# Expert gates on Trainium2: four fp32 one-hot products per group against twelve in bf16

## The chip, the cores and the metric

The kernel runs on one core of one Trainium2 chip. The metric is the time of one execution on the device in microseconds (us). Engines: TensorE (PE for matmuls, PEld for the loads of its stationary operand), VectorE (DVE), ScalarE (ACT), GpSimd (POOL), and SyncE (SP), whose queue issues most DMAs.

## The reference, cut to what matters

Two layers run over x (256 tokens by 1024). Each is an attention mixer followed by a retrieval among 16,384 = 128 x 128 experts. The retrieval, cut:

```
v1, i1 = top_k(sc[:, :, 0], 16)            # per token and head (8 heads)
v2, i2 = top_k(sc[:, :, 1], 16)
cand     = v1[..., :, None] + v2[..., None, :]
top_v, pos = top_k(cand, 16)
eidx     = i1 * 128 + i2 at pos
gates    = softmax(top_v)
a   = gelu(u_tab[eidx] . x) * gates
out = sum over the 8 x 16 chosen: a * v_tab[eidx]
```

The kernel gathers nothing. It multiplies every token with all 128 tiles of u, weights the result with a dense gate array, and multiplies with all 128 tiles of v. The gate array G[i2, i1, t] holds for each token t the gate of expert (i1, i2), and zero where that expert wasn't chosen. It is built as matrix products. For a token, the 128 choices (8 heads x 16) lie on the partitions. A matrix A[choice, n] = (n == one index of the choice) and a matrix B[choice, n] = gate of the choice where n == its other index give, as A transposed times B, the 128 x 128 gate block of that token.

## The kernel before, in words

Each layer ends in `experts(l)`. Its stages, in the order in which PE does them:

- Up products, 128 steps. Step n takes a tile of u (128 x 1024 fp32), which ACT copies in two halves into `hi` (rounded to fp32r, `split`, L967), and DVE subtracts to `lo` (`lower`, L1338). PE then does 24 products of 256 columns into one bank (`up`: hi by x_hi, hi by x_lo, lo by x_hi for each of 8 slices). ACT applies gelu into `work` (L973), and SP stores it to DRAM (`spill`). `hi` and `lo` have two slots each, so the split of step n+2 waits for the products of step n.
- During the steps up to 55, DVE finds the choices (`retrieve_head`, `choose`). After step 53, PE runs `picks`: 64 bf16 products that turn the indices so that choices lie on partitions (bank 6), and two fp32 transposes of the gates (bank 7). DVE copies these into `pick` (L1401, L1402): three rows of 256 tokens, fp32, for the two indices and the gate.
- Steps 56 to 119 each have a group of four tokens besides. DVE builds the one-hots of group g (`one_hot`, L1340): one TENSOR_TENSOR compares `iota` with the first index for four tokens (128 x 512, L1343), and four TENSOR_SCALAR, one a token, compare with the second index and multiply by the gate (128 x 128 each, L1346). It goes into one of two buffers `hot`. PE does the four fp32 products of the group after its up step (`group`, L747) into bank g % 4. ACT copies the bank into the gate array (`copy_gates`, L989). In DVE's program, a group stands after the two `lower` halves of a step. `one_hot(g)` waits until the products of group g-2 are done, `group(g)` waits for `hot_ready` g+1 and for the copy of group g-4.
- Steps 120 to 127 are up products alone. Then come the 128 down steps (`down`): weigh, split, and 12 products of 512 columns for a tile of v.

In the trace each fp32 product of a token shows as two matmul instructions with two weight loads: 1024 of them for 512 products. A product of fp32r or bf16 operands shows as one.

All three memory areas of the change lie in `wmod_ring` (3 x 1024 fp32 a partition). Its first two thirds are `hot`, its last third is first `pick` and later `back`, the area that fetches the stored gelu results once all 64 groups are done. In layer 0, it also takes tiles of w_mod before the groups begin and after they end.

The order is written out by hand: each engine has its own program, and semaphores tie them. `link` on DVE means that the next instruction waits for this one through a semaphore.

Of the kernel before, what the change touches and what calls it, by code (L numbers as in the profile page):

```python
# [8 lines left out]
ALU = mybir.AluOpType  # L9
# [3 lines left out]
BF16 = mybir.dt.bfloat16  # L13
# [3 lines left out]
P = 128  # L17
D = 1024
KT = D // P
T = 256  # L20
# [45 lines left out]
def win_cols(l):  # L66

    return QK_TILES[l] * KT * P + sum(V_WIDTHS[l]) * KT + (GATE_COLS * KT if l == 0 else 0)
# [11 lines left out]
KEYS_AT = QS_AT + 2 * 2 * T  # L80
OUT_AT = KEYS_AT
BIG = P * T
WIN_TILES = win_cols(1) // D
PIECE = D

# [65 lines left out]
def build(nc, a, out):  # L151

    with ExitStack() as ctx:
        def sb(name, shape, dt=F32):
            return ctx.enter_context(nc.sbuf_tensor(name, shape, dt))
# [3 lines left out]

        big = sb("big", [P, BIG])  # L160
        raw = sb("raw", [P, RAWS, D])
# [8 lines left out]
        wmod_ring = sb("wmod_ring", [P, MODS, D])  # L170
# [2 lines left out]
        c_all = sb("c_all", [P, D])  # L173
        work = sb("work", [P, 4, T])
        stat = sb("stat", [P, 256])
        pick = wmod_ring[:, 2, 0:3 * T].rearrange("p (a t) -> p a t", a=3)

        first_mods = [wmod_ring[:, n] for n in range(MODS)]
        first_mods += [big[:, V_AT + n * D:V_AT + (n + 1) * D] for n in range(TT)]
# [2 lines left out]
        first_mods += [big[:, n * D:(n + 1) * D] for n in range(LATE_MODS)]  # L182
        fox_maps = wmod_ring[:].rearrange("p a n -> p (a n)")

        hot = [x.rearrange("p (a t n) -> p a t n", a=2, n=P) for x in (wmod_ring[:, 0], wmod_ring[:, 1])]
        back = wmod_ring[:, 2].rearrange("p (r t) -> p r t", t=T)
        bank = [ctx.enter_context(nc.psum_tensor(f"bank{i}", [P, 512], F32)) for i in range(8)]

# [2 lines left out]
        iota = cst[:, C_IOTA:C_IOTA + P]  # L191
# [64 lines left out]
        def q_area(at, size, **kw):  # L256
# [48 lines left out]
                 "map_ps", "map_max", "neg_ready", "exp_done", "prob_ready", "pt_ps", "pt_copied", "av_ps", "av_copied",  # L305
                 "y_ps", "x_mixed",
                 "q_ps", "q_copied", "key_ps", "key_copied", "equal_ready", "sel_ready", "pick_copied",
                 "hot_ready", "hot_used", "g_copied", "hi_done", "lo_done", "w_used",
                 "s_gelu", "a_ready", "ah_done", "al_done",
                 "e_copied", "eT_ps", "x_done")  # L310
        s = [{n: sem(f"{n}_{l}") for n in names} for l in range(LAYERS)]
# [136 lines left out]
        def _(pool):  # L448
            for l in range(LAYERS):
# [26 lines left out]
                else:  # L476
                    pool.wait_ge(s[1]["wt_used"], 2 * WIN_TILES)
                pool.dma_start(big[:, WOUT_AT:WOUT_AT + KT * D], a["w_out"][l]).then_inc(wout_in, 16)
# [11 lines left out]
        def _(pe):  # L490
            def mm(o, w, x, start=True, stop=True, free=False):
                return nc.tensor.matmul(o, w, x, start=start, stop=stop, skip_group_check=free)  # L492
# [15 lines left out]
            def project_split():  # L508

                def open_half(w, h):  # L510
                    if h == 0 and w < QK_TILES[1] and w % 4 == 0:
                        pe.wait_ge(win_in[w // 4], loads_in(1, min(4, QK_TILES[1] - w) * D))
                    if h == 0 and w == QK_TILES[1]:
                        pe.wait_ge(win_in[4], loads_in(1, KT * V_WIDTHS[1][0]))
                    if h == 0 and w == WIN_TILES - 1:
                        pe.wait_ge(win_in[5], loads_in(1, KT * V_WIDTHS[1][1]))
# [213 lines left out]
            def experts(l):  # L730

                def up(n, r, wait=True):

                    if wait:
                        pe.wait_ge(s[l]["s_gelu"], n - 1)
                    o = bank[4 + r][:, 0:T]
                    for h in range(2):
                        pe.wait_ge(s[l]["hi_done"], 2 * n + h + 1)
                        pe.wait_ge(s[l]["lo_done"], 2 * n + h + 1)
                        for k in range(h * KT // 2, (h + 1) * KT // 2):  # L740
                            c = slice(k * P, (k + 1) * P)
                            mm(o, hi[:, r, c], x_hi[:, k, :], k == 0, False)
                            mm(o, hi[:, r, c], x_lo[:, k, :], False, False)
                            last = mm(o, lo[:, r, c], x_hi[:, k, :], False, k == KT - 1)
                        last.then_inc(s[l]["w_used"], 1)

                def group(g, b, wait=True):  # L747

                    if wait:
                        pe.wait_ge(s[l]["g_copied"], g - 3)  # L750
                    pe.wait_ge(s[l]["hot_ready"], g + 1)
                    for n in range(4):
                        last = mm(bank[b][:, n * P:(n + 1) * P], hot[b % 2][:, 0, n, :], hot[b % 2][:, 1, n, :])
                    last.then_inc(s[l]["hot_used"], 1)

                def down(j, r, first=False, end=False):

                    pe.wait_ge(s[l]["ah_done"], j + 1)
                    pe.wait_ge(s[l]["al_done"], j + 1)
                    for h in range(2):  # L760
                        pe.wait_ge(s[l]["hi_done"], STREAM + 2 * j + h + 1)
                        pe.wait_ge(s[l]["lo_done"], STREAM + 2 * j + h + 1)
                        c = slice(h * HALF, (h + 1) * HALF)
                        for t in range(TT):
                            o, tok = bank[2 * t + h][:, :], slice(t * P, (t + 1) * P)
                            mm(o, a_hi[:, r, tok], hi[:, r, c], first, False, True)
                            mm(o, a_hi[:, r, tok], lo[:, r, c], False, False, True)
                            last = mm(o, a_lo[:, r, tok], hi[:, r, c], False, end, True)
                        last.then_inc(s[l]["w_used"], 1)

                pe.wait_ge(s[l]["xh_done"], l + 1)
                pe.wait_ge(s[l]["xl_done"], l + 1)
                up(0, 0, False)
                up(1, 1, False)
                with pe.Fori(1, GROUP_AT // 2 - 1) as i:
                    for r in range(2):
                        up(2 * i + r, r)
                picks(l)
                for r in range(2):
                    up(GROUP_AT - 2 + r, r)  # L780
                for r in range(4):
                    up(GROUP_AT + r, r % 2)
                    group(r, r, False)
                with pe.Fori(1, GROUPS // 4) as i:
                    for r in range(4):
                        up(GROUP_AT + 4 * i + r, r % 2)
                        group(4 * i + r, r)
                with pe.Fori((GROUP_AT + GROUPS) // 2, NKEY // 2) as i:
                    for r in range(2):
                        up(2 * i + r, r)  # L790
                pe.wait_ge(s[l]["g_copied"], GROUPS)
                down(0, 0, first=True)
                with pe.Fori(0, NKEY // 2 - 1) as i:
                    for r in range(2):
                        down(2 * i + 1 + r, 1 - r)
                down(NKEY - 1, 1, end=True)
# [12 lines left out]
            for k in range(KT):  # L809
                last = mm(bank[1 + k // 4][:, (k % 4) * P:(k % 4 + 1) * P], silu8[:, k:k + 1].to_broadcast([P, P]), ident)  # L810
# [21 lines left out]
        def _(act):  # L832
# [101 lines left out]
            for l in range(LAYERS):  # L934
# [83 lines left out]
                act.wait_ge(s[l]["gate_max"], l + 1)  # L1018
                f(q_e[:], q_e[:], ACT.Exp).then_inc(s[l]["gate_exp"], 1)
                up_steps(32, GROUP_AT)  # L1020
                act.wait_ge(s[l]["pick_copied"], 2)
                with act.Fori(0, GROUPS // 4) as i:
                    for r in range(4):
                        up_step(GROUP_AT + 4 * i + r, r, i + GROUP_AT // 4)
# [25 lines left out]
        def _(dve):  # L1050
            steps = [0]

            def link(ins):
                steps[0] += 1
                ins.then_inc(dve_step, 1)
                dve.wait_ge(dve_step, steps[0])

            v = nc.vector
# [274 lines left out]
            def experts(l):  # L1333
# [6 lines left out]
                def one_hot(g, r, wait=True):  # L1340
                    if wait:
                        dve.wait_ge(s[l]["hot_used"], g - 1)
                    v.tensor_tensor(hot[r % 2][:, 0], iota.unsqueeze(1).to_broadcast([P, 4, P]),  # L1343
                                    pick[:, 0, bass.ds(4 * g, 4)].unsqueeze(2).to_broadcast([P, 4, P]), ALU.is_equal)
                    for n in range(4):
                        ins = v.tensor_scalar(hot[r % 2][:, 1, n, :], iota, pick[:, 1, bass.ds(4 * g + n, 1)],  # L1346
                                              pick[:, 2, bass.ds(4 * g + n, 1)], ALU.is_equal, ALU.mult)
                    ins.then_inc(s[l]["hot_ready"], 1)

                def weigh(j, b, round_):  # L1350
                    dve.wait_ge(s_in[b], 16 * (round_ + 1) + 16 * l * (NKEY // STAGES))
# [46 lines left out]
                for _ in left:  # L1398
                    pass
                dve.wait_ge(s[l]["pick_ps"], l + 1)  # L1400
                v.tensor_copy(pick[:, 0:2, :].rearrange("p a b -> p (a b)"), bank[6][:, :]).then_inc(s[l]["pick_copied"], 1)  # L1401
                v.tensor_copy(pick[:, 2, :], bank[7][:, 0:T]).then_inc(s[l]["pick_copied"], 1)  # L1402
                dve.wait_ge(s[l]["pick_copied"], 2)
                for g in range(4):
                    for half in range(2):
                        lower(GROUP_AT + g, g, half)
                    one_hot(g, g, g >= 2)
# [40 lines left out]


            dve.wait_ge(const_in, 16)  # L1450
            v.tensor_copy(ident_bf, ident).then_inc(ident_ready, 1)
            dve.wait_ge(silu_e, 1)
            link(v.tensor_scalar(silu8, silu8, 1.0, None, ALU.add))
# [6 lines left out]
            for l in range(LAYERS):  # L1460
# [14 lines left out]
                if l == 0:  # L1475
                    dve.wait_ge(par_in, 16)
                    for n in range(2):
                        ins = v.tensor_tensor_reduce(stat[:, n * HD:(n + 1) * HD], lam_in[:, 2 * n, :], lam_in[:, 2 * n + 1, :], 1.0, 0.0,
                                                     ALU.mult, ALU.add, lam[:, n:n + 1])
# [31 lines left out]
                for m in range(KT):  # L1511
                    dve.wait_ge(s[l]["eT_ps"], m // 2 + 1)
                    c = (m % 2) * T
# [97 lines left out]
```

## Time and profile before

| | |
|---|---|
| median of 3 runs | 2069.59 us (2067.72 to 2069.62) |
| profiled execution, its own time | 2068.17 us |
| its span, first to last instruction | 2066.2 us |
| PE busy | 2001.3 us (97%) |
| DVE busy | 1488.5 us (72%) |
| ACT busy | 1054.0 us (51%) |
| granted TensorE clock, mean | 0.981 |

The span is what the profiler sees of the instructions, 2.0 us less than the execution's own time. A busy share is an average over the whole span. "x" numbers are counts of instructions. In a timeline the first column is the start in us, the second the length from the start of the first to the end of the last of a merged row. Matmuls are pipelined, so their lengths overlap and what a matmul costs PE is the distance between two starts.

### The profile page before, as it was taken

The page shows a single profiled execution, that of the slowest core. Times are in us where ns is not written, and L with a number is a line of the kernel's source. Part 1 is how long each engine was busy: PE and PEld are TensorE (multiplying, and loading weights), DVE is VectorE, ACT ScalarE, POOL GpSimd, SP SyncE. Part 2 cuts the span into 40 slices and gives each one's busy share as a digit, 9 for nine tenths or more (in the row PEclk, how much of TensorE's full clock was granted, in tenths as well). Part 3 has the DMA queues.
Part 4 walks back from the last instruction along what each step waited for, and adds up shares of the span by engine and source line. Part 5 has one row for each costly group of instructions (what it writes and reads, how often), then busy time and mean ns, then how long its engine had stood idle before and what let it go on. Part 6 is the DMA issues. An engine that isn't in the chain of part 4 may idle for free.

```text
span 2066.2 us, 43340 instructions
## 1 busy us (share of the span) xinstructions
PE 2001.3 (97%) x12616; PEld 1792.2 (87%) x12616; DVE 1488.5 (72%) x3743; ACT 1054.0 (51%) x2059; POOL 27.7 (1%) x56
## 2 busy tenths in 40 slices
PE   5989999999999999999999899999999999999997
PEld 4847899999999877777779689999999998888886
DVE  5663778877777688888875348886777767777776
ACT  2032245755555555555554423566555555555554
POOL 0000000000000000000000000000000000000000
PEclk7999999999999999999989999999999999999999
DMA  9861279865556899999830324877565677777774
GB/s 377 333 234 42 101 272 288 254 192 174 171 176 177 269 329 327 317 333 321 279 106 31 153 106 125 228 219 214 176 174 170 176 207 244 240 241 241 241 241 152
DMA packets 170903, 446.77 MB, mean 216 GB/s; under 512 B 19024, under 2 KB 85840, under 8 KB 166880
## 3 DMA queue, kind: packets, MB, share of 16 engines
q1 hardware_dynamic: 163472, 392.65, 60.0%
q0 software_dynamic: 7376, 53.45, 6.7%
q8 instruction: 27, 0.44, 0.1%
q14 instruction: 28, 0.23, 0.0%
HBM read 409.32 MB, written 36.70 MB: 216 GB/s over the span
## 4 chain that ended last, share of the span: by engine, by line
PE 94%; ACT 2%; DVE 2%; DMA 1%; issue 1%; DVEq 0%; ACTq 0%; SPq 0%
PE bank L492 93%; ACT big L913 1%; DMA big<-in_w_mod 1%; PE bank L626 1%; DVE raw L1079 0%; DVE big L1174 0%; DVE big L1096 0%; DVE wmod_ring L1096 0%; DVE x_lo L1088 0%; ACT hi L871 0%; ACT L973 0%; ACT big L931 0%; DMA cst<-in_consts 0%; PE bank L803 0%; ACT raw L860 0%
## 5 line engine op out<-in xcount | busy, mean ns | idle before, releaser
L1338 DVE TENSOR_TENSOR lo<-raw,hi 128x512 fp32r<-128x512 f32 x1024 | 702.8, 690 | 346.6 <-ACT hi L967 342.3
L967 ACT ACTIVATE hi<-raw 128x512 fp32r<-128x512 f32 x1024 | 642.6, 629 | 445.3 <-PE bank L492 433.2
L492 PE MATMUL bank<-x_hi,hi 128*128 128x256 f32 x2152 | 623.1, 290 | 3.6 <-ACT work L973 1.6
L492 PE MATMUL bank<-x_hi,lo 128*128 128x256 f32 x2152 | 610.7, 284 | 0.0
L492 PE MATMUL bank<-x_lo,hi 128*128 128x256 f32 x2152 | 606.2, 283 | 0.0
L492 PEld LDWEIGHTS bank<-x_hi,hi 128*128 128x128 f32 x2152 | 414.1, 192 | 6.4 <-issue 4.5
L492 PEld LDWEIGHTS bank<-x_hi,lo 128*128 128x128 f32 x2152 | 414.3, 193 | 0.0
L492 PEld LDWEIGHTS bank<-x_lo,hi 128*128 128x128 f32 x2152 | 411.8, 192 | 0.0
L492 PE MATMUL bank<-hi,a_hi 128*128 128x512 f32 x1024 | 401.1, 392 | 3.4 <-issue 2.1
L492 PE MATMUL bank<-hi,a_lo 128*128 128x512 f32 x1024 | 398.8, 389 | 0.0
L492 PE MATMUL bank<-lo,a_hi 128*128 128x512 f32 x1024 | 398.6, 389 | 0.0
L492 PE MATMUL bank<-raw,big 128*128 128x256 f32 (+1 forms) x1040 | 238.8, 388 | 17.8 <-ACT raw L860 17.8
L492 PEld LDWEIGHTS bank<-raw,big 128*128 128x128 f32 (+1 forms) x1040 | 196.4, 192 | 50.4 <-issue 22.6
L492 PEld LDWEIGHTS bank<-hi,a_hi 128*128 128x128 f32 x1024 | 192.2, 188 | 54.5 <-issue 13.3
L492 PEld LDWEIGHTS bank<-hi,a_lo 128*128 128x128 f32 x1024 | 192.2, 188 | 40.5
L492 PEld LDWEIGHTS bank<-lo,a_hi 128*128 128x128 f32 x1024 | 192.2, 188 | 39.0
L973 ACT ACTIVATE work<-bank 128x256 f32<-128x256 f32 x256 | 98.1, 383 | 188.0 <-PE bank L492 186.9
L1346 DVE TENSOR_SCALAR wmod_ring<-cst,wmod_ring 128x128 f32<-128x128 f32 x512 | 142.4, 342 | 0.0
L492 PE MATMUL bank<-wmod_ring 128*128 128x128 f32 x1024 | 135.1, 275 | 0.0
L492 PEld LDWEIGHTS bank<-wmod_ring 128*128 128x128 f32 x1024 | 125.7, 192 | 0.0
L995 ACT ACTIVATE a_hi<-wmod_ring 128x256 fp32r<-128x256 f32 x256 | 103.5, 404 | 11.4 <-DVE wmod_ring L1352 10.6
L1352 DVE TENSOR_TENSOR wmod_ring<-wmod_ring,big 128x256 f32<-128x256 f32 x256 | 107.2, 419 | 1.8 <-issue 0.4
(157 smaller groups left out, 1305.3 us busy)
## 6 DMA issues: line engine op xcount, KB each, us to landing
raw<-in_u SPq DMA_DIRECT2D x256, 512.0 KB, 3.9
raw<-in_v SPq DMA_DIRECT2D x256, 512.0 KB, 4.6
s_store<-work SPq DMA_DIRECT2D x256, 128.0 KB, 3.7
wmod_ring<-s_store SPq DMA_DIRECT2D x256, 128.0 KB, 3.7
wmod_ring<-in_w_mod SPq DMA_DIRECT2D x54, 512.0 KB, 5.8
big<-in_w_mod SPq DMA_DIRECT2D x40, 512.0 KB, 6.2
big<-in_w_q POOLq DMA_DIRECT2D x16, 1024.0 KB, 6.3
big<-in_w_in POOLq DMA_DIRECT2D x6, 2048.0 KB, 13.4
```

Source lines behind the costliest of these rows:

```text
L492: return nc.tensor.matmul(o, w, x, start=start, stop=stop, skip_group_check=free)
L626: last = nc.tensor.transpose(bank[4 + n % 2][:, c * P:(c + 1) * P], scores[:, i, c * P:(c + 1) * P], ident)
L913: last = f(c, c, ACT.Exp, bias=neg[:, 2 * i + t:2 * i + t + 1], accum_out=den[:, 2 * i + t:2 * i + t + 1])
L967: f(hi[:, r % 2, c], raw[:, r, c], ACT.Copy).then_inc(s[l]["hi_done"], 1)
L973: f(work[:, r, :], bank[4 + r % 2][:, 0:T], ACT.Gelu).then_inc(s[l]["s_gelu"], 1)
L995: f(a_hi[:, r % 2, :], back[:, b, :], ACT.Copy).then_inc(s[l]["ah_done"], 1)
L1338: v.tensor_tensor(lo[:, r % 2, c], raw[:, r, c], hi[:, r % 2, c].bitcast(F32), ALU.subtract).then_inc(s[l]["lo_done"], 1)
L1346: ins = v.tensor_scalar(hot[r % 2][:, 1, n, :], iota, pick[:, 1, bass.ds(4 * g + n, 1)], pick[:, 2, bass.ds(4 * g + n, 1)], ALU.is_equal, ...
L1352: v.tensor_tensor(back[:, b, :], back[:, b, :], gates[:, bass.ds(j, 1), :].rearrange("p a t -> p (a t)"), ALU.mult)\
```

## The change

A gate value is cut into three bf16 pieces whose sum is the fp32 value: its bf16 rounding, the bf16 rounding of what is left, and what is left then. The one-hots (zeros and ones) are bf16. B becomes three bf16 matrices, one a piece, and the block of a token is the sum of three bf16 products in one bank. So a group has 12 bf16 products in place of 4 in fp32.

The buffer of a group is laid out as [5 matrices][128 indices n][4 tokens], with the four tokens innermost. Both operands of each product are therefore read with a step of four elements, 8 bytes. VectorE builds it with two instructions: one compares a table `iota4` (each index four times) with both indices of the four tokens (128 x 1024, output bf16), the other multiplies the second one-hot by the three pieces (128 x 1536, bf16). The second reads what the first wrote, so it waits for it (`hot_plain`).

Once a layer, before the groups: the pick copy now writes bf16, and the pieces take two subtractions and three roundings of 256 columns, each waiting for the one before it where it reads its output. ACT, ahead of its first group, waits for one more count of `pick_copied`. Once in the kernel, at the very start, `iota4` is written (128 x 512, bf16).

```
@@ -80,6 +80,7 @@
 OUT_AT = KEYS_AT
 BIG = P * T
+HOT = 5 * 4 * P // 2
 WIN_TILES = win_cols(1) // D
@@ -173,7 +174,11 @@
         stat = sb("stat", [P, 256])
-        pick = wmod_ring[:, 2, 0:3 * T].rearrange("p (a t) -> p a t", a=3)
+        iota4 = sb("iota4", [P, P, 4], BF16)
+        pick_bf = sb("pick_bf", [P, 2, T], BF16)
+        ring = wmod_ring[:].rearrange("p a n -> p (a n)")
+        gate_bf = ring[:, 2 * HOT:2 * HOT + 3 * T // 2].bitcast(BF16).rearrange("p (a t) -> p a t", a=3)
+        gate_left = ring[:, 0:T]
@@ -182,7 +187,7 @@
-        hot = [x.rearrange("p (a t n) -> p a t n", a=2, n=P) for x in (wmod_ring[:, 0], wmod_ring[:, 1])]
+        hot = [ring[:, n * HOT:(n + 1) * HOT].bitcast(BF16).rearrange("p (a n t) -> p a n t", a=5, t=4) for n in range(2)]
@@ -305,7 +310,7 @@
-                 "hot_ready", "hot_used", "g_copied", "hi_done", "lo_done", "w_used",
+                 "hot_plain", "hot_ready", "hot_used", "g_copied", "hi_done", "lo_done", "w_used",
@@ -750,7 +755,8 @@
                     for n in range(4):
-                        last = mm(bank[b][:, n * P:(n + 1) * P], hot[b % 2][:, 0, n, :], hot[b % 2][:, 1, n, :])
+                        for c in range(3):
+                            last = mm(bank[b][:, n * P:(n + 1) * P], hot[b % 2][:, 0, :, n], hot[b % 2][:, 2 + c, :, n], c == 0, c == 2)
                     last.then_inc(s[l]["hot_used"], 1)
@@ -1018,7 +1024,7 @@
-                act.wait_ge(s[l]["pick_copied"], 2)
+                act.wait_ge(s[l]["pick_copied"], 3)
@@ -1340,12 +1346,13 @@
                 def one_hot(g, r, wait=True):
                     if wait:
                         dve.wait_ge(s[l]["hot_used"], g - 1)
-                    v.tensor_tensor(hot[r % 2][:, 0], iota.unsqueeze(1).to_broadcast([P, 4, P]),
-                                    pick[:, 0, bass.ds(4 * g, 4)].unsqueeze(2).to_broadcast([P, 4, P]), ALU.is_equal)
-                    for n in range(4):
-                        ins = v.tensor_scalar(hot[r % 2][:, 1, n, :], iota, pick[:, 1, bass.ds(4 * g + n, 1)],
-                                              pick[:, 2, bass.ds(4 * g + n, 1)], ALU.is_equal, ALU.mult)
-                    ins.then_inc(s[l]["hot_ready"], 1)
+                    v.tensor_tensor(hot[r % 2][:, 0:2], iota4[:].unsqueeze(1).to_broadcast([P, 2, P, 4]),
+                                    pick_bf[:, :, bass.ds(4 * g, 4)].unsqueeze(2).to_broadcast([P, 2, P, 4]), ALU.is_equal)\
+                        .then_inc(s[l]["hot_plain"], 1)
+                    dve.wait_ge(s[l]["hot_plain"], g + 1)
+                    v.tensor_tensor(hot[r % 2][:, 2:5], hot[r % 2][:, 1:2].to_broadcast([P, 3, P, 4]),
+                                    gate_bf[:, :, bass.ds(4 * g, 4)].unsqueeze(2).to_broadcast([P, 3, P, 4]), ALU.mult)\
+                        .then_inc(s[l]["hot_ready"], 1)
@@ -1398,9 +1405,14 @@
                 dve.wait_ge(s[l]["pick_ps"], l + 1)
-                v.tensor_copy(pick[:, 0:2, :].rearrange("p a b -> p (a b)"), bank[6][:, :]).then_inc(s[l]["pick_copied"], 1)
-                v.tensor_copy(pick[:, 2, :], bank[7][:, 0:T]).then_inc(s[l]["pick_copied"], 1)
+                v.tensor_copy(pick_bf[:].rearrange("p a b -> p (a b)"), bank[6][:, :]).then_inc(s[l]["pick_copied"], 1)
+                v.tensor_copy(gate_bf[:, 0, :], bank[7][:, 0:T]).then_inc(s[l]["pick_copied"], 1)
                 dve.wait_ge(s[l]["pick_copied"], 2)
+                v.tensor_tensor(gate_left, bank[7][:, 0:T], gate_bf[:, 0, :], ALU.subtract).then_inc(s[l]["pick_copied"], 1)
+                dve.wait_ge(s[l]["pick_copied"], 3)
+                link(v.tensor_copy(gate_bf[:, 1, :], gate_left))
+                link(v.tensor_tensor(gate_left, gate_left, gate_bf[:, 1, :], ALU.subtract))
+                link(v.tensor_copy(gate_bf[:, 2, :], gate_left))
@@ -1448,6 +1460,7 @@
             dve.wait_ge(const_in, 16)
+            v.tensor_copy(iota4[:], iota.unsqueeze(2).to_broadcast([P, P, 4]))
             v.tensor_copy(ident_bf, ident).then_inc(ident_ready, 1)
```

## Rows read from the trace of the kernel before

**Rows 1.** The page: busy time of each engine, and the chain's shares by engine

```profile
PE 2001.3 (97%) x12616; PEld 1792.2 (87%) x12616; DVE 1488.5 (72%) x3743; ACT 1054.0 (51%) x2059; POOL 27.7 (1%) x56
...
PE 94%; ACT 2%; DVE 2%; DMA 1%; issue 1%; DVEq 0%; ACTq 0%; SPq 0%
```

**Rows 2.** Windows: stretch, its length, busy PE, PEld, DVE, ACT, POOL, PEclk, DMA, GB/s

```profile
436.40:682.20 245.80, 245.80 (x2089) 245.80 (x2089) 187.25 (x445) 138.88 (x262) 0.00 (x0) 1.00 0.60 175
1430.80:1676.60 245.80, 245.80 (x2089) 245.80 (x2089) 190.03 (x453) 137.88 (x259) 0.00 (x0) 1.00 0.60 174
```

**Rows 3.** PE's timeline over one step with its group

```profile
560.77 1.06 PE L492 MATMUL bank<-wmod_ring 128*128 128x128 f32 x8
561.58 0.36 PE L492 MATMUL bank<-x_hi,hi 128*128 128x256 f32 x1
561.78 0.28 PE L492 MATMUL bank<-x_lo,hi 128*128 128x256 f32 x1
561.90 0.28 PE L492 MATMUL bank<-x_hi,lo 128*128 128x256 f32 x1
...
564.54 1.06 PE L492 MATMUL bank<-wmod_ring 128*128 128x128 f32 x8
```

**Rows 4.** PE and its weight loads by shape, whole span: count | busy us, mean ns

```profile
L492 PE MATMUL bank<-wmod_ring 128*128 128x128 f32 x1024 | 135.1, 275 | 0.0
L492 PEld LDWEIGHTS bank<-wmod_ring 128*128 128x128 f32 x1024 | 125.7, 192 | 0.0
...
L492 PE MATMUL bank<-par,big 128*128 128x128 bf16 x128 | 7.5, 219 | 0.0
L492 PEld LDWEIGHTS bank<-par,big 128*128 128x128 bf16 x128 | 7.2, 98 | 0.1
```

**Rows 5.** PE's timeline over the picks of layer 0

```profile
424.02 3.75 PE L492 MATMUL bank<-par,big 128*128 128x128 bf16 x64
427.61 0.39 PE L727 MATMUL bank<-cst,big 128*128 128x128 f32 x2
```

**Rows 6.** DVE's timeline over one step with its group

```profile
561.91 0.69 DVE L1338 TENSOR_TENSOR lo<-raw,hi 128x512 fp32r<-128x512 f32 x1 [0.76 <-ACT hi L967]
562.51 0.68 DVE L1343 TENSOR_TENSOR wmod_ring<-cst,wmod_ring 128x512 f32<-128x512 f32 x1
563.12 1.11 DVE L1346 TENSOR_SCALAR wmod_ring<-cst,wmod_ring 128x128 f32<-128x128 f32 x4
564.14 0.69 DVE L1338 TENSOR_TENSOR lo<-raw,hi 128x512 fp32r<-128x512 f32 x1
```

**Rows 7.** DVE by shape: the nearest rows to the two new instructions

```profile
L1324 DVE TENSOR_TENSOR big<-big 128x512 bf16<-128x512 bf16 x32 | 21.9, 684 | 0.0
L1502 DVE TENSOR_TENSOR x_lo<-raw,x_hi 128x2048 fp32r<-128x2048 f32 x2 | 4.6, 2291 | 5.1 <-ACT x_hi L960 5.1
L1310 DVE CAST big<-big 128x512 f32<-128x512 uint32 x2 | 0.8, 421 | 0.0
```

**Rows 8.** DVE's timeline around the pick copy of layer 0

```profile
428.03 0.69 DVE L1401 COPY wmod_ring<-bank 128x512 f32<-128x512 f32 x1 [2.19 <-PE bank L727]
428.64 0.41 DVE L1402 COPY wmod_ring<-bank 128x256 f32<-128x256 f32 x1
430.20 0.69 DVE L1338 TENSOR_TENSOR lo<-raw,hi 128x512 fp32r<-128x512 f32 x1 [1.15 <-ACT hi L967]
```

**Rows 9.** The start of the kernel: timeline of DVE and PE

```profile
3.69 0.23 DVE L1451 CAST par<-cst 128x128 bf16<-128x128 f32 x1 [3.69 <-DMA cst<-in_consts]
3.83 0.16 DVE L1453 TENSOR_SCALAR stat<-stat 128x8 f32<-128x8 f32 x1
4.03 0.20 DVE L1454 RECIPROCAL stat<-stat 128x8 f32<-128x8 f32 x1
4.26 0.17 DVE L1455 TENSOR_TENSOR stat<-stat 128x8 f32<-128x8 f32 x1
```

**Rows 10.** Window: a stretch of up steps without groups, layer 1

```profile
1330.00:1420.00 90.00, 89.20 (x744) 89.03 (x743) 68.34 (x136) 61.12 (x106) 0.00 (x0) 1.00 0.78 224
```

## The prediction

> **What bounds the kernel now.** I read the page first for the engine that carries the chain [rows 1]: PE is busy 97% of the span and 94% of the chain is its. A share over the whole span doesn't say that the stage of the groups is like that, so next come the windows over the two layers' group stages [rows 2]: PE is busy in all of 245.80 us of each, at the full granted clock (1.00), while DVE is busy 76 to 77%, ACT 56% and the DMA engines 60%. In this stage nothing but the distance between PE's starts counts. PE's timeline gives it [rows 3]: groups begin at 560.77 and 564.54, a period of 3.77 us. The 24 products of an up step start 0.12 us apart (561.78, 561.90), 2.88 us in all. The rest, 3.767 - 2.88 = 0.887 us, is the group. It holds eight fp32 instructions. The merged row is 1.06 us long and one is 275 ns [rows 4], so they start (1.06 - 0.275) / 7 = 0.112 us apart, and eight make 0.90. The reader is to see that 0.887 is this and nothing else: no idle time stands ahead of the group or behind it. There are 64 such groups a layer, 128 in all: 114 us of the kernel.
>
> **PE, the term that decides.** Removed: 128 x 0.887 us. Added: 12 bf16 products of 128 columns a group. The trace has the same shape in one place, the picks: 64 products in a merged row of 3.75 us [rows 5], each 219 ns long [rows 4], so (3.75 - 0.219) / 63 = 0.056 us from start to start, each with its own weight load (98 ns, against 192 ns for one in fp32 [rows 4]). Twelve make 0.673 us. There the operands lie packed. Here both step by 8 bytes, and no row shows a strided read by PE. Its bounds: 0.056 us if the step is free, and from the nearest slower row 0.112 us, as if each column took the two passes' time that it takes in fp32.
>
> I take 0.056. The products of the up step, fp32r, already read 4 bytes a column at one column per PE cycle (256 columns in 0.120 us), and a bf16 weight load is far shorter than the fp32 one. So there is some room on both reads, but how much isn't shown, and this is the weakest step. By the Trainium skill, page "Advanced Engine Details and Errata", section "SBUF Cachelines", SBUF is read in lines of 16 bytes, and two hits in a line are enough to hide the access: with 8 bytes a step there are just two, so by it the step is free and the sum stays at 0.673 us, at the very edge of the rule. No row here shows it.
>
> Another page speaks against the change. The Trainium skill, "TensorE: Matmul & The Clock Gate", section "Back-to-back issue gap", gives about 81 ns a matmul for a stream of weight load and matmul pairs of 128 columns. By that, twelve would take 0.97 us and the kernel would get slower by some 11 us. The row of the picks, 56 ns with a load each [rows 5], disagrees.
>
> There is a seam besides. The first product of the next up step needs a weight load of 192 ns, and ahead of it now stands a short product instead of an fp32 one. Below: nothing, as at the old seam, where the block's 0.887 us is less than eight times 0.112. Above: what the fp32 load is longer than the bf16 one, 0.19 - 0.10 = 0.09 us. I take 0.03. The new block is then 0.70 us, the period 3.58, and the saving 128 x (0.887 - 0.703) = 23.6 us; with the seam's two bounds it is 27.4 to 15.9 us.
>
> **DVE, which must stay below PE.** Its timeline [rows 6]: in a period two `lower` of 0.60 us start to start, one compare of 0.61, four TENSOR_SCALAR in 1.02, together 2.84 of 3.77 us, the rest idle behind ACT. So DVE's saving, if there is one, is worth nothing; what counts is whether the new pair stays under what PE leaves. The pair covers 1024 and 1536 elements. Bounds from rows: at one element a cycle, 2048 elements took 2291 ns and 512 took 684 [rows 7], that is 158 ns + 1.042 ns an element, so 1.225 and 1.758 us. At two a cycle, as the cast of 512 words in 421 ns shows the engine can go for one input (0.52 ns an element), 0.69 and 0.96 us. The second waits for the first through a semaphore: a linked instruction starts about 0.035 us after the end of the one before (3.83 + 0.16 to 4.03 [rows 9]), while an unlinked one starts 0.08 us before it. Per period:
>
> - two a cycle: 1.21 + 0.69 + 0.035 + 0.96 - 0.08 = 2.82 us, hidden under 3.58;
> - one a cycle: 1.21 + 1.225 + 0.035 + 1.758 - 0.08 = 4.15 us, over both the new and the old period.
>
> The nearest row, L1324, is a TENSOR_TENSOR with bf16 output and runs at one a cycle (684 ns for 512), but its second input, `numbers`, is fp32 in the code. Here all three are 2 bytes and the innermost run has step 1. Two such elements are the 4 bytes which each stream already moves a cycle in the fp32 rows (512 in 0.68 us [rows 6]), so no more bytes pass than the rows show. I take two a cycle, with both ends kept. The Trainium skill says the same on page "VectorE: DVE Perf Modes", section "The perf-mode tier table": TENSOR_TENSOR doubles its rate with bf16 operands in SBUF and not with fp32 ones; by it the first of the two sums holds. If only the second instruction ran at one a cycle, the sum would be 1.21 + 0.73 + 1.68 = 3.62 us: PE would wait 0.04 us a group and most of the gain would stay.
>
> **Waits and queues.** Behind the new wait on DVE stand the second instruction and then the `lower` of the next step. `hot_ready` comes two groups ahead of its use (DVE had finished a group at 564.23, and PE takes that one some 4 us later, the next but one [rows 3, 6]), and the `lower` has to be done only two steps after the slot came free. ACT does the same two splits, one gelu and one bank copy, 56% of 3.77 us, 2.1 us a period [rows 2]. SP issues the same DMAs, now every 3.58 us, which raises their rate from 175 to some 184 GB/s. A stretch of bare up steps moves 224 GB/s with PE 99% busy [rows 10], so the loads follow.
>
> **Once a layer.** The pick copy [rows 8] takes 428.03 to 429.05. With the subtractions and roundings, four more of at most 0.42 us and 0.035 each, DVE is done near 430.9. The next `lower`, which starts at 430.20, slips 0.7 us. Its step's products start at 436.47 - 2.88 = 433.6 us, two us after it then ends. Cost zero; without that cover 1.9 us a layer. ACT reaches the wait for `pick_copied` 3 only after step 55, long past 430.
>
> **Once in the kernel.** `iota4` stands ahead of the cast and of the three small instructions that PE waits for [rows 9]. 512 elements: 0.34 to 0.61 us start to start (from 421 and 684 ns less 0.08). The queue of w_mod tiles behind may take in some of it. I take +0.4; bounds 0 and 0.6.
>
> **Sum.** 2068.17 (this execution's own time) - 23.6 + 0.4 = 2045.0 us. The median of the runs is 1.4 us above the profiled execution, so I forecast 2046 us. Within this case the seam and the start give 2041 to 2055.
>
> **Rivals.**
>
> - Strided reads cost PE the second cycle a column, 0.112 us a product. The block is 12 x 0.112 = 1.35 us, 0.46 more than now, over 128 groups +59 us: 2129. Decisive point: 0.887 / 12 = 0.074 us a product is break-even; above it the kernel is slower. For it: no strided read in the trace, both operands at once strided. Against: bf16 columns are half as wide as those that PE streams at full rate. Chance 0.14.
> - Something between, 0.06 to 0.081 us a product: loads that no longer fully hide, or a step that costs a part. At 0.065 it is 2060 with the seam, at 0.081, the figure of the page named above, 2081 without it: +10.9. Chance 0.13, of which 0.06 is faster, 0.03 within the bound of no change and 0.04 slower.
> - DVE runs one element a cycle in both instructions and sets the period at 4.15 us: (4.15 - 3.767) x 128 = +49, 2119. It decides from a DVE sum of 3.77 us. For it: the row of L1324. Against: its fp32 input. Chance 0.06.
> - The forecast, PE at 0.056 and DVE hidden: chance 0.67.
>
> That PE isn't the limit and the change therefore moves nothing I exclude by [rows 2].
>
> **How the numbers follow.** Faster: 0.67 + 0.06 = 0.73. Within 0.2% (4 us, about what a measurement of this kernel can tell from no change): 0.03. Slower: 0.04 + 0.14 + 0.06 = 0.24. The range leaves out the two slow rivals, together 0.20, and so runs from 2039 (the whole seam gone, and a little) to 2085 us. The likeliest case's own is 2041 to 2055.
>
> **What would show it.** In the new profile's PE timeline a merged row of 12 bf16 products would be (0.219 + 11 x 0.056) = 0.84 us long, groups 3.58 us apart, and the stage 229 us a layer in place of 241. A row of 1.45 us and a period of 4.2 would be the strided read. DVE: the group of the compare at 0.69 us and of the multiply at 0.96 us; at 1.2 and 1.76 us it is the third rival, with PE then waiting for DVE's `wmod_ring` in each group. The window's clock should stay at 1.00. The forecast falls if PE starts are spaced above 0.074 us, or if idle time shows ahead of the group.

## The result, and the profile after

The changed kernel takes 2133.26 us (median of 4 runs, 2132.36 to 2134.36) against 2068.91 us before: a ratio of 1.031, with a 95% interval of 1.0295 to 1.0325. It is 64 us slower. The profiled execution took 2132.36 us with a span of 2130.4 us.

The page first, as in [rows 1], then the window over the groups of layer 0, as in [rows 2]:

```profile
PE 2068.4 (97%) x13128; PEld 1851.6 (87%) x13128; DVE 1494.4 (70%) x3368; ACT 1055.1 (50%) x2059; POOL 27.7 (1%) x56
...
436.40:711.20 274.80, 274.80 (x2305) 270.86 (x2305) 186.08 (x254) 136.70 (x256) 0.00 (x0) 1.00 0.52 154
```

PE is still busy without a gap in the stage of the groups and at the full granted clock (1.00). VectorE is busy for less of it than before (186.08 of 274.80 us). So nothing new waits: the same engine has more to do. Its timeline over one step, against [rows 3]:

```profile
560.95 0.28 PE L497 MATMUL bank<-x_hi,lo 128*128 128x256 f32 x1
561.08 1.58 PE L497 MATMUL bank<-wmod_ring 128*128 128x128 bf16 x12
562.41 0.37 PE L497 MATMUL bank<-x_hi,hi 128*128 128x256 f32 x1
562.62 0.28 PE L497 MATMUL bank<-x_lo,hi 128*128 128x256 f32 x1
...
565.38 1.58 PE L497 MATMUL bank<-wmod_ring 128*128 128x128 bf16 x12
```

The groups begin 4.30 us apart, not 3.77. The block is 4.30 - 2.88 = 1.42 us, against 0.887. By shape, to be held against [rows 4]:

```profile
L497 PE MATMUL bank<-wmod_ring 128*128 128x128 bf16 x1536 | 202.5, 296 | 0.0
...
L497 PEld LDWEIGHTS bank<-wmod_ring 128*128 128x128 bf16 x1536 | 163.4, 118 | 7.7
```

The merged row gives (1.58 - 0.296) / 11 = 0.117 us from start to start. The bf16 product of the picks, same shape and type but packed operands, took 219 ns and 0.056 from start to start [rows 4, 5]. Each product is longer by 77 ns and each weight load by 20 ns. From these rows alone either could set the pace.

VectorE's timeline over a step, against [rows 6]:

```profile
562.21 0.69 DVE L1344 TENSOR_TENSOR lo<-raw,hi 128x512 fp32r<-128x512 f32 x1 [1.02 <-ACT hi L973]
562.82 0.68 DVE L1349 TENSOR_TENSOR wmod_ring<-iota,pick_bf 128x1024 bf16<-128x1024 bf16 x1
563.64 0.96 DVE L1353 TENSOR_TENSOR wmod_ring<-wmod_ring 128x1536 bf16<-128x1536 bf16 x1
564.80 0.69 DVE L1344 TENSOR_TENSOR lo<-raw,hi 128x512 fp32r<-128x512 f32 x1 [0.20 <-ACT hi L973]
```

1024 elements in 0.68 us and 1536 in 0.96: two elements a cycle, and VectorE waits more than before ahead of `lower`. The pick copy, against [rows 8], and the start, against [rows 9]:

```profile
428.04 0.69 DVE L1408 CAST pick_bf<-bank 128x512 bf16<-128x512 f32 x1 [2.19 <-PE bank L732]
...
430.34 0.29 DVE L1415 CAST wmod_ring<-wmod_ring 128x256 bf16<-128x256 f32 x1
430.67 0.69 DVE L1344 TENSOR_TENSOR lo<-raw,hi 128x512 fp32r<-128x512 f32 x1
```

```profile
3.75 0.43 DVE L1463 CAST iota<-cst 128x512 bf16<-128x512 f32 x1 [3.75 <-DMA cst<-in_consts]
...
4.67 0.17 DVE L1468 TENSOR_TENSOR stat<-stat 128x8 f32<-128x8 f32 x1
```

The `lower` behind the picks starts at 430.67 in place of 430.20, and the first group still begins at 436.5. The start is 0.41 us later at this point and nothing of it is left at the first group.

From the first to the last product of the groups, layer 0 takes 271.9 us (436.5 to 708.4) against 238.1, layer 1 272.0 (1469.7 to 1741.7) against 238.1. That is +67.7 us, and the span grew by 64.2. Of the other 3.5 us, 3.2 came back between the two stages: from the last product of layer 0's groups to the first of layer 1's it was 764.5 us (674.6 to 1439.1), and it is 761.3 (708.4 to 1469.7). Some 2 us of them lie before the end of layer 0's down steps (the last copy of layer 0's output by ACT starts 31.75 us later than before, where the groups had left a lag of 33.8). There PE is idle for 3.5 us before (712.0 to 1058.4) and for 1.6 after (746.0 to 1090.2). Up to that copy every run below is shorter than the kernel before as well, by 1.2 us in run 8 and by 2.1 or 2.2 in the others, with packed operands too. So against the one trace of before this part goes with the change and not with the step of the reads. The prediction has no term for it, and its cause stays open. The rest varies from run to run.

### The profile page after: what moved, and what is told of

Read it like the earlier page. It is cut to its first block, busy times and chain, and to the rows that moved or that the text cites. A ratio compares the mean times of both kernels' runs of the same rounds, so it can differ in the third digit from the quotient of the medians.

```text
span 2130.4 us, 43749 instructions
## 1 busy us (share of the span) xinstructions
PE 2068.4 (97%) x13128; PEld 1851.6 (87%) x13128; DVE 1494.4 (70%) x3368; ACT 1055.1 (50%) x2059; POOL 27.7 (1%) x56
## 4 chain that ended last, share of the span: by engine, by line
PE 94%; ACT 2%; DVE 1%; DMA 1%; issue 1%; SPq 0%; ACTq 0%; DVEq 0%
PE bank L497 93%; ACT big L919 1%; DMA big<-in_w_mod 1%; PE bank L631 1%; DMA raw<-in_v 0%; DVE raw L1085 0%; DVE big L1180 0%; DVE big L1102 0%; DVE wmod_ring L1102 0%; DVE x_lo L1094 0%; ACT hi L877 0%; ACT L979 0%; DMA cst<-in_consts 0%; ACT big L937 0%; PE bank L809 0%
## 5 line engine op out<-in xcount | busy, mean ns | idle before, releaser
L497 PE MATMUL bank<-wmod_ring 128*128 128x128 bf16 x1536 | 202.5, 296 | 0.0
L497 PEld LDWEIGHTS bank<-wmod_ring 128*128 128x128 bf16 x1536 | 163.4, 118 | 7.7
L1353 DVE TENSOR_TENSOR wmod_ring<-wmod_ring 128x1536 bf16<-128x1536 bf16 x128 | 122.6, 958 | 17.4
L995 ACT ACTIVATE big<-bank 128x512 f32 x128 | 76.7, 599 | 75.2 <-PE bank L497 75.2
```

The source lines that it names most:

```text
L995: f(dst, bank[b][:, :].rearrange("p (t j) -> p j t", t=4), ACT.Copy).then_inc(s[l]["g_copied"], 1)
L1353: v.tensor_tensor(hot[r % 2][:, 2:5], hot[r % 2][:, 1:2].to_broadcast([P, 3, P, 4]), gate_bf[:, :, bass.ds(4 * g, 4)].unsqueeze(2).to_broa ...
```

## The experiments

**What the experiments change.** Where a run is said to have wrong values, the products read other addresses of the same buffer, so the gate array isn't the reference's; instructions, counts, shapes and waits stay. An operand with a step of 8 or 16 elements, and the moving one in layer 0 of run 7, is read from one place in all products of a group. Runs 2, 3 and 5 to 8 are one execution each; what is read from them are distances and clocks within a trace. One helper serves them (`flat` is the buffer of a group as 2560 bf16 elements):

```
+        def cut(b, at, step):
+            return flat[b][:, at:at + step * P].rearrange("p (n t) -> p n t", t=step)[:, :, 0] if step > 1 else flat[b][:, at:at + P]
```

**1. Both operands packed.**

```
-  last = mm(bank[b][:, n * P:(n + 1) * P], hot[b % 2][:, 0, :, n], hot[b % 2][:, 2 + c, :, n], c == 0, c == 2)
+  last = mm(bank[b][:, n * P:(n + 1) * P], cut(b % 2, n * P, 1), cut(b % 2, 1024 + n * P, 1), c == 0, c == 2)
```

> Both operands of the 12 bf16 products are read packed (128 adjacent elements of the same buffer), so the gate array holds wrong values; everything else is as in the changed kernel. Theory S (the 8-byte step of the operands is the whole loss): products 0.056 us apart as in the picks, a block of 0.67 to 0.76 us, groups 3.58 us apart, total near 2045 us, faster than before by about 24. Rival C (the loss lies in the products' number, in the three that accumulate into the same columns, or in their place between fp32r products, not in the step): blocks stay at 1.42 us, total near 2132.

Measured: 2045.57 us, ratio to the kernel before 0.9889 (0.9873 to 0.9906). PE's timeline:

```profile
562.40 0.84 PE L501 MATMUL bank<-wmod_ring 128*128 128x128 bf16 x12
563.06 0.36 PE L501 MATMUL bank<-x_hi,hi 128*128 128x256 f32 x1
...
566.02 0.84 PE L501 MATMUL bank<-wmod_ring 128*128 128x128 bf16 x12
```

One product is 220 ns in this stage, so (0.84 - 0.220) / 11 = 0.056 us. The groups stand 3.62 us apart. The step of the operands is the whole loss, and more: without it the change wins 23 us. Rival C is out. In this run the three products of a token read the same elements; run 4 will show the same pace with three different pieces.

**2. One operand packed at a time.** Same edit, with steps (1, 4) for (stationary, moving) in layer 0 and (4, 1) in layer 1.

> One operand packed at a time, values wrong for it: in layer 0 the stationary operand is packed and the moving one keeps its 8-byte step; in layer 1 it is the other way round. Theory M (the moving read sets the pace): groups 4.30 us apart in layer 0 and 3.58 in layer 1. Theory W (the weight load sets it): 3.58 in layer 0 and 4.30 in layer 1. If either step alone is enough, 4.30 in both and a total near 2132; else near 2089.

Measured: 2086.14 us. PE's timeline, layer 0 and then layer 1, and the shapes in a window of each:

```profile
563.83 1.55 PE L501 MATMUL bank<-wmod_ring 128*128 128x128 bf16 x12
...
1560.59 0.86 PE L501 MATMUL bank<-wmod_ring 128*128 128x128 bf16 x12
...
1564.21 0.86 PE L501 MATMUL bank<-wmod_ring 128*128 128x128 bf16 x12
```

```profile
L501 PE MATMUL bank<-wmod_ring 128*128 128x128 bf16 x593 | 76.7, 293 | 0.0
L501 PEld LDWEIGHTS bank<-wmod_ring 128*128 128x128 bf16 x591 | 62.0, 113 | 2.2
...
L501 PE MATMUL bank<-wmod_ring 128*128 128x128 bf16 x564 | 40.5, 221 | 0.0
L501 PEld LDWEIGHTS bank<-wmod_ring 128*128 128x128 bf16 x564 | 33.2, 115 | 2.0
```

With the moving operand alone at 8 bytes, a product starts every (1.55 - 0.293) / 11 = 0.114 us. With the stationary one alone, every (0.86 - 0.221) / 11 = 0.058, and the period is 3.62 us. Theory M holds. It isn't quite all: with both at 8 bytes a product took 0.117 us, and the groups of layer 0 took 271.9 us against 269.2 here (436.2 to 705.4). So of the 0.061 us that a product lost, 0.058 belong to the moving operand, and the stationary one's step costs the other 2.7 us a layer. The load takes 113 ns in the first case too, where its operand is packed: so its extra length isn't its own step alone.

**3. Steps of 4 and of 16 bytes, both operands.** Steps (2, 2) in layer 0, (8, 8) in layer 1.

> Both operands read at a step of two elements (4 bytes) in layer 0 and of eight (16 bytes) in layer 1, values wrong. Theory N (a step of one 4-byte word is free, a longer one costs): groups 3.58 us apart in layer 0. Theory A (any step but one costs the double): 4.30 in layer 0. Layer 1: if the cost is a fixed doubling, 4.30; if it grows with the bytes stepped over, a product takes twice 0.117 us, 12 of them 2.8 us, and the groups stand about 5.7 us apart.

Measured: 2243.27 us. PE's timeline in layer 0, then in layer 1, and the windows over part of layer 1's groups, over one block and over the up products behind it:

```profile
562.94 0.86 PE L501 MATMUL bank<-wmod_ring 128*128 128x128 bf16 x12
...
1562.11 3.00 PE L501 MATMUL bank<-wmod_ring 128*128 128x128 bf16 x12
1564.74 0.48 PE L501 MATMUL bank<-x_hi,hi 128*128 128x256 f32 x1
...
1566.57 0.41 PE L501 MATMUL bank<-x_hi,hi 128*128 128x256 f32 x1
1566.78 0.41 PE L501 MATMUL bank<-x_lo,hi 128*128 128x256 f32 x1
...
1569.31 3.00 PE L501 MATMUL bank<-wmod_ring 128*128 128x128 bf16 x12
```

```profile
1500.00:1700.00 200.00, 200.00 (x1054) 170.66 (x1053) 88.59 (x118) 62.72 (x118) 0.00 (x0) 0.81 0.32 95
...
1562.10:1564.70 2.60, 2.60 (x14) 1.66 (x12) 0.69 (x1) 0.91 (x2) 0.00 (x0) 1.00 0.00 0
...
1565.00:1569.20 4.20, 4.20 (x25) 4.20 (x23) 2.34 (x3) 1.23 (x2) 0.00 (x0) 0.59 0.55 156
```

At 4 bytes a product costs (0.86 - 0.219) / 11 = 0.058 us: theory N. At 16 bytes, one is 415 ns long and starts every (3.00 - 0.415) / 11 = 0.235 us: twice the cost at 8 bytes, as the growing version said. Its 5.7 us a period was too low: this period is 7.20 us (1562.11 to 1569.31), and the mean over layer 1 is 6.73 (64 groups, first to last product 1425.7 to 1852.2). The rest is in the up products behind the block: they start 0.21 us apart (1566.57 to 1566.78) for most of the step where they took 0.12 at the full clock. The granted clock of the stretch is 0.81, a mean over parts at 2.4 GHz and parts at 1.2 GHz: it is 1.00 in the block and 0.59 over the up products behind it. It fell although PE counts as busy throughout.

**4. Two tokens innermost: the version that follows.** The buffer is laid out as [10][128][2], and the pick copies write group by group so that VectorE still needs two instructions. It computes the reference.

```
-  hot: rearrange("p (a n t) -> p a n t", a=5, t=4)
+  hot: rearrange("p (a n t) -> p a n t", a=10, t=2)
-  hot[b % 2][:, 0, :, n],      hot[b % 2][:, 2 + c, :, n]
+  hot[b % 2][:, n // 2, :, n % 2], hot[b % 2][:, 4 + 2 * c + n // 2, :, n % 2]
-  v.tensor_tensor(hot[r % 2][:, 0:2], iota4 ... [P, 2, P, 4], pick_bf[:, :, bass.ds(4 * g, 4)] ...
+  v.tensor_tensor(hot[r % 2][:, 0:4], iota2 ... [P, 4, P, 2], pick_bf[:, bass.ds(8 * g, 8)] as [4][2] ...
```

(The table keeps its name `iota4` in the code and is half as long, `iota2` above. The multiply and the writes of the pieces are laid out alike and not shown.)

> Computes the reference. The buffer holds two tokens innermost instead of four, so both operands are read at a step of 4 bytes; VectorE still builds it in two instructions with innermost runs of two. Theory N: products 0.056 us apart, total 2045 us, faster than before. Theory A: total near 2132. VectorE: 0.69 and 0.96 us if runs of two keep two elements a cycle, else 1.2 and 1.76 us, which with fast products would give groups 4.15 us apart and 2117 us.

Measured: 2047.05 us, ratio 0.9896 (0.9879 to 0.9912). PE's and VectorE's timeline:

```profile
562.96 0.86 PE L498 MATMUL bank<-wmod_ring 128*128 128x128 bf16 x12
...
566.58 0.86 PE L498 MATMUL bank<-wmod_ring 128*128 128x128 bf16 x12
```

```profile
564.70 0.69 DVE L1350 TENSOR_TENSOR wmod_ring<-iota,pick_bf 128x1024 bf16<-128x1024 bf16 x1
565.55 0.96 DVE L1354 TENSOR_TENSOR wmod_ring<-wmod_ring 128x1536 bf16<-128x1536 bf16 x1 [0.16 <-DVE wmod_ring L1350]
```

Runs of two keep VectorE at two elements a cycle, and PE no longer pays. This is the change as it was forecast, in the layout that keeps it.

**5. The law of the moving read: 6 and 32 bytes.** Stationary packed, moving at 3 elements in layer 0 and 16 in layer 1.

> Stationary operand packed, moving operand at a step of three elements (6 bytes) in layer 0 and of sixteen (32 bytes) in layer 1, values wrong. So far moving steps of 4, 8 and 16 bytes gave 0.058, 0.114 and 0.235 us a product. Theory R (the time goes with the bytes stepped over, about 0.44 ns for 4 bytes): 0.086 us in layer 0 and 0.47 in layer 1. Theory L (the time goes with the 16-byte lines touched, at most one a column, 1.8 ns each): also 0.086 in layer 0, but 0.235 again in layer 1. Rival D (free up to 4 bytes, then double and double again): 0.114 in layer 0.

Measured: 2211.36 us. PE's timeline, layer 0, layer 1:

```profile
563.41 1.23 PE L501 MATMUL bank<-wmod_ring 128*128 128x128 bf16 x12
...
1562.26 2.94 PE L501 MATMUL bank<-wmod_ring 128*128 128x128 bf16 x12
```

One product is 252 and 410 ns long: (1.23 - 0.252) / 11 = 0.089 us, (2.94 - 0.410) / 11 = 0.230. Theory L. At 32 bytes it costs no more than at 16. At 0.089 the groups of layer 0 stand 3.96 us apart, against 3.77 before the change.

**6. The stationary operand at 16 and 32 bytes,** moving packed.

> Moving operand packed, stationary operand at a step of eight elements (16 bytes) in layer 0 and of sixteen (32 bytes) in layer 1, values wrong. At 8 bytes a load grew from 98 to 115 ns and stayed hidden (0.058 us a product). Theory H (the weight load reads several parts at once and hides at any step): 0.06 us in both layers, total near 2050. Rival: the load itself becomes the pace at 16 bytes, with products 0.08 us apart or more and groups over 3.9 us apart.

Measured: 2061.07 us, neither of the two. PE's timeline and the loads, layer 0, layer 1:

```profile
564.54 0.96 PE L501 MATMUL bank<-wmod_ring 128*128 128x128 bf16 x12
...
568.27 0.96 PE L501 MATMUL bank<-wmod_ring 128*128 128x128 bf16 x12
```

```profile
L501 PEld LDWEIGHTS bank<-wmod_ring 128*128 128x128 bf16 x636 | 43.7, 149 | 2.3
...
L501 PEld LDWEIGHTS bank<-wmod_ring 128*128 128x128 bf16 x576 | 39.9, 150 | 2.1
```

The load grew to 149 ns and almost hides: a product starts every (0.96 - 0.230) / 11 = 0.066 us, the groups every 3.73. The total lies 11 us above what theory H said and well below the rival's.

**7. Is it the step, or the blocks of 16 bytes?** Runs of neighbours, one run in each 16 bytes: two columns a run in layer 0, four in layer 1.

```
+        def runs(b, at, run):
+            return flat[b][:, at:at + 8 * P // run].rearrange("p (n t) -> p n t", t=8)[:, :, 0:run]
...
+  x = runs(b % 2, 1024, 2) if l == 0 else runs(b % 2, 1024 + n * P, 4)
```

> Stationary operand packed; the moving operand's innermost step is one element, but its 128 columns are spread over 16-byte lines: 64 runs of two neighbours, one run a line, in layer 0, and 32 runs of four neighbours, one run a line, in layer 1. Values wrong. Theory L (a product costs 1.8 ns for each 16-byte line touched, and no less than 0.056 us): 64 lines give 0.114 us in layer 0, as the 8-byte step did, and 32 lines give 0.058 in layer 1. Rival E (what counts is whether neighbouring columns lie next to each other): 0.056 to 0.06 in both layers. Rival J (each jump costs, whatever it spans): 64 jumps cost 0.085 or so in layer 0 and 0.07 in layer 1.

Measured: 2087.88 us. PE's timeline, layer 0, layer 1:

```profile
560.90 1.55 PE L504 MATMUL bank<-wmod_ring 128*128 128x128 bf16 x12
...
1620.10 0.87 PE L504 MATMUL bank<-wmod_ring 128*128 128x128 bf16 x12
```

One product is 293 and 220 ns long: 0.114 and 0.059 us. Theory L again. Half of the neighbours adjacent doesn't help; how many 16-byte blocks the row of 128 columns touches does.

All moving reads together, stationary operand packed except at 4 bytes (run 3); "blocks" counts the 16-byte blocks touched:

| moving operand | blocks | us a product | 1.8 ns x blocks |
|---|---|---|---|
| packed | 16 | 0.056 | 0.029 |
| step 4 bytes | 32 | 0.058 | 0.058 |
| four neighbours in 16 bytes | 32 | 0.059 | 0.058 |
| step 6 bytes | 48 | 0.089 | 0.086 |
| step 8 bytes | 64 | 0.114 | 0.115 |
| two neighbours in 16 bytes | 64 | 0.114 | 0.115 |
| step 16 bytes (run 8) | 128 | 0.225 | 0.230 |
| step 32 bytes | 128 | 0.230 | 0.230 |

**8. Where the rest of the 7.2 us period came from.** Steps (8, 8) in layer 0, (1, 8) in layer 1.

> Both operands at a step of 16 bytes in layer 0, the moving one alone in layer 1 (stationary packed), values wrong. It asks where the unexpected part of the 7.2 us period came from that both gave in layer 1 before: there the granted clock fell to 0.81 and the up products ran at 0.21 us for half of the step. If that goes with the load of the stationary operand: layer 0 at 7.2 us a period with the clock near 0.8, layer 1 at 5.7 with the clock near 1.0, products 0.235 us apart in both. If it goes with the layer or with chance: layer 0 near 5.7, layer 1 near 7.2, or both alike.

Measured: 2401.57 us. Windows over the groups of layer 0 and of layer 1, and PE's timeline in layer 1:

```profile
436.40:860.00 423.60, 423.60 (x2239) 361.49 (x2238) 189.36 (x251) 133.02 (x250) 0.00 (x0) 0.81 0.33 97
1632.00:2008.00 376.00, 376.00 (x2259) 297.07 (x2258) 188.53 (x250) 133.38 (x250) 0.00 (x0) 0.92 0.38 110
```

```profile
1703.26 2.88 PE L501 MATMUL bank<-wmod_ring 128*128 128x128 bf16 x12
...
1708.86 2.88 PE L501 MATMUL bank<-wmod_ring 128*128 128x128 bf16 x12
1711.39 0.54 PE L501 MATMUL bank<-x_hi,hi 128*128 128x256 f32 x1
1711.72 0.42 PE L501 MATMUL bank<-x_lo,hi 128*128 128x256 f32 x1
...
1715.96 2.88 PE L501 MATMUL bank<-wmod_ring 128*128 128x128 bf16 x12
```

Both operands at 16 bytes give 0.81 in either layer. The moving one alone gives 0.92: a period is 5.60 us where the clock stays up (1703.26 to 1708.86), near the 5.7 expected, and 7.10 where it falls behind the block (1708.86 to 1715.96). So the extra time is the clock. It fell in the stages whose moving reads step by 16 or 32 bytes and stayed at 1.00 over the groups at every faster pace, and with the stationary operand's step it falls more often (0.81 against 0.92). In the changed kernel's groups it didn't fall (1.00). What in such reads lowers it, and why the stationary operand matters to it, stays open.

**9. Two pieces instead of three,** on top of run 4.

```
-                        for c in range(3):
+                        for c in range(2):
-                link(v.tensor_tensor(gate_left, gate_left, gate_bf[:, 1, :], ALU.subtract))
-                link(v.tensor_copy(gate_bf[:, 2, :], gate_left))
```

> The layout with two tokens innermost (4-byte step) and only two bf16 pieces of the gate instead of three, so the gate's last eight bits are left out: eight products a group. If the distance between PE's starts is still all that counts, four products of 0.058 us less in each of 128 groups save 30 us more: 2047 - 30 = 2017 us. Rival: VectorE or the splits take over as the limit of the stage, since the period would be 3.39 us; then less than 30, above all idle time of PE ahead of the up steps.

Measured: 2019.44 us, ratio 0.9758 (0.9745 to 0.9771).

```profile
561.02 0.63 PE L498 MATMUL bank<-wmod_ring 128*128 128x128 bf16 x8
...
564.42 0.63 PE L498 MATMUL bank<-wmod_ring 128*128 128x128 bf16 x8
```

The period is 3.40 us and PE still doesn't wait. The saving over run 4 is 27.6 us of the 30 expected. It is the fastest version, at the price of a gate that is rounded to two pieces.

## Why the prediction was wrong, step by step

- **The step that failed** is "I take 0.056": the cost of one bf16 product whose operands step by 8 bytes. It is 0.117 us, above even the upper bound of 0.112 that I had taken from the fp32 rows, and runs 1 and 2 put 0.058 of the 0.061 us between on the moving operand. Everything behind it follows: 12 x 0.117 = 1.40 us, a block of 1.42, and 128 x (1.42 - 0.887) = 68 us of loss in place of 23.6 of gain. The first rival had named the strided read and priced it at 2129 us; it got 0.14. Its price came near because the cost at 8 bytes happens to be the double: "the second cycle a column" isn't the mechanism, since 128 columns cost 0.058 us at 4 bytes and 0.235 at 16 (run 3).
- **The argument for it** was that fp32r products read 4 bytes a column at full rate, so a bf16 read had "some room". The room is there, but it is counted in 16-byte blocks touched, not in bytes used: 4 bytes a column, packed in fp32r or stepped in bf16, touch one block for four columns, and that is just free (0.058 us). 8 bytes touch twice as many, and that is double.
- **The rule that I leaned on beside it.** The Trainium skill, "Advanced Engine Details and Errata", section "SBUF Cachelines", says that at least two hits on a line are needed to absorb the access latency. I read it as: two are enough. The block of 16 bytes is confirmed (32 bytes cost the same as 16, run 5). Two hits weren't enough for the moving operand: 0.114 us against 0.056. Four were.
- **The rule that spoke against.** The 81 ns of the Trainium skill, "TensorE: Matmul & The Clock Gate", section "Back-to-back issue gap", isn't seen in any run here: packed pairs of load and product went at 0.056 us also between fp32r products (run 1).
- **Break-even** at 0.074 us left out the seam. With the seam as measured, 0.06 us, it is (0.887 - 0.06) / 12 = 0.069. At 0.066 the groups stood 3.73 us apart and the total was 2061 (run 6), below the kernel before; at 0.089 they stood 3.96 apart (run 5, layer 0), above the 3.77 before.
- **The seam** was taken as 0.03 us. In run 1 the block is 3.62 - 2.88 = 0.74 us and the products make 12 x 0.056 = 0.67, so it is some 0.06: inside the bounds, worth 4 us.
- **The total with packed operands** came out at 2045.6 us against the forecast of 2046 (run 1), and that is luck in part. Its groups saved 19.6 us (228.3 us a layer in place of 238.1) where the sum had 23.6. The span shrank by 23.9 us because of the 4.3 us outside the groups, 3.7 of them the gain between the two stages that stays unexplained.
- **The low end of 2041** leaves out the 1.4 us between the profiled execution and the median: 2068.17 - 27.4 + 1.4 = 2042. Nothing hangs on it.
- **VectorE** was right: 0.68 and 0.96 us against 0.69 and 0.96, two elements a cycle, hidden. The wait between them costs 0.14 us (562.82 + 0.68 to 563.64), not 0.035. It is hidden too.
- **Once a layer, once in the kernel:** DVE done at 430.6 against 430.9 predicted, no cost on the path. `iota4` 0.41 us at the start, taken as 0.4, but none of it is left at the first group.
- **What was wrong in the weighing:** the sign hung on the only step without a row, and the forecast still got 0.67. The steps with rows missed by little: 4 us at the seam, and a wait on VectorE that stayed hidden. The rival that this step left open cost two and a half times what the forecast won.

## What to carry to other kernels

A layout that pleases the engine that writes a buffer must be priced on the engine that reads it, and where that reader sets the end, its read comes first: here VectorE had 0.9 us of idle time a step to give, and PE none. Keep PE's moving operand at four or more columns per 16 bytes. Here, with 128 bf16 columns, a step was free up to that (0.058 us against 0.056), so two bf16 tokens interleaved serve both engines. If the step on which the sign depends has no row in the trace, look for what would be needed to stay clear of it, or give its bad end a larger chance.

## What the runs showed of the hardware that was not expected

- The moving read costs 1.8 ns for each 16-byte block that the columns touch, with 0.056 us as the floor for 128 columns; the two patterns tried at 32 blocks cost the same, and so do the two at 64 (runs 2, 3, 5, 7, 8).
- The stationary read is far more tolerant: with the moving operand packed a load took 98 ns packed, 115 at 8 bytes, 149 at 16 and 150 at 32, and a product slowed from 0.056 to only 0.066 us (runs 1, 2, 6).
- With slow reads the granted clock came down although PE counts as busy all the time: 0.81 with both operands at 16 bytes, in two runs, and 0.92 and 0.97 with the moving one alone at 16 and 32 (runs 3, 8, 5). The up products behind such a block then run at 1.2 GHz (0.21 us apart instead of 0.12).
